# Expert weights with consecutive contraction rows on a partition, and strided stationary tiles to match, in a one-core encoder block

## What is computed

```
def _hier_moe(h, w_rg, b_rg, w_re, b_re, w_gate, w_up, w_down):
    t = h.reshape(b * s, d)                       # 512 tokens x 1024
    g_idx = argmax over 4 groups; top_i = the best 2 of the group's 8 experts
    combine = weight of each token for each of the 32 experts (two are not zero)
    for gi in range(N_EXPERT_GROUPS):
        hg = jnp.einsum('td,edf->tef', t, w_gate[gi])      # 1024 -> 256 per expert
        hu = jnp.einsum('td,edf->tef', t, w_up[gi])
        act = silu(hg) * hu * combine[:, gi, :, None]
        out = out + jnp.einsum('tef,efd->td', act, w_down[gi])   # 256 -> 1024
```

## Time and profile before

| | us |
|---|---|
| median of 3 runs | 947.07 |
| lowest and highest | 946.57, 948.12 |
| span of the profiled execution, first to last instruction | 947.1 |
| PE busy in it | 840.8 |
| expert stage, first fetch to last `down` | 590.5 to 903.0 |

### The profile page before, as it was taken

One profiled execution on the slowest core, in us unless ns is written; L12 is line 12 of the kernel. 1 busy time (PEld: TensorE's weight loads), 2 busy tenths in 40 slices (PEclk: granted clock), 3 DMA queues, 4 the chain that ended last, 5 costly groups with the idle time before them and its releaser, 6 DMA issues.

```text
span 947.1 us, 11294 instructions
## 1 busy us (share of the span) xinstructions
PE 840.8 (89%) x4489; PEld 584.5 (62%) x4489; DVE 426.3 (45%) x780; ACT 176.5 (19%) x331; POOL 151.3 (16%) x74
## 2 busy tenths in 40 slices
PE   0599997799999999999999998999999999999910
PEld 0488787788888885444448887756565556555600
DVE  6999534455688883112365763112111211121128
ACT  4222223453232220000002010111111111111112
POOL 6734741110123111000004000000000000000032
PEclk9999998899999999999999999999999999999965
DMA  9524231111121226230007462359999999999452
GB/s 307 193 90 89 82 97 45 45 45 46 46 78 56 57 78 233 78 126 31 21 0 253 148 206 106 97 201 359 357 357 371 361 360 356 367 363 358 153 183 106
DMA packets 119296, 163.42 MB, mean 173 GB/s; under 512 B 14412, under 2 KB 102614, under 8 KB 118742
## 3 DMA queue, kind: packets, MB, share of 16 engines
q1 hardware_dynamic: 113184, 139.68, 45.1%
q0 software_dynamic: 3072, 12.63, 3.7%
q10 hardware_dynamic: 2998, 10.53, 2.8%
HBM read 148.15 MB, written 14.68 MB: 172 GB/s over the span
## 4 chain that ended last, share of the span: by engine, by line
PE 83%; DVE 8%; DMA 4%; ACT 2%; issue 2%; POOL 0%; ACTq 0%; SPq 0%; DVEq 0%; POOLq 0%
PE psum L732 23%; PE psum L1010 14%; PE psum L1022 12%; PE psum L1037 6%; PE psum L941 6%; PE psum L931 6%; PE psum L980 4%; PE psum L922 3%; DMA ring<-in_w_in_dram 2%; DVE arena L1378 2%; ACT arena L1090 2%; DVE arena L1377 2%; PE psum L871 2%; PE psum L891 1%; PE psum L982 1%
## 5 line engine op out<-in xcount | busy, mean ns | idle before, releaser
L732 PE MATMUL psum<-ring_r 128*128 128x512 f32 (+1 forms) x768 | 213.2, 363 | 2.6 <-DVE arena L1549 1.3
L732 PEld LDWEIGHTS psum<-ring_r 128*128 128x128 f32 x768 | 139.4, 194 | 26.1 <-issue 2.4
L1010 PEld LDWEIGHTS psum<-arena 128*128 128x128 f32 x1088 | 125.5, 194 | 28.4 <-issue 25.1
L1010 PE MATMUL psum<-arena 128*128 128x128 f32 x1088 | 131.6, 280 | 2.9 <-DVE arena L1702 2.9
L667 POOL TENSOR_TENSOR ring_r<-ring,ring_r 128x2048 fp32r<-128x2048 f32 x20 | 93.4, 4670 | 205.3 <-ACT ring_r L1090 205.3
L1090 ACT COPY arena<-psum 128x512 f32<-128x512 f32 (+3 forms) x104 | 58.5, 582 | 351.8 <-PE psum L948 139.8
L1022 PE MATMUL psum<-ring,arena 128*64 128x512 f32 x512 | 113.4, 595 | 7.9 <-ACT arena L1090 7.9
L732 PE MATMUL psum<-arena_r,ring_r 128*128 128x512 f32 x256 | 100.4, 392 | 0.0
L1797 DVE SCALAR_TENSOR_TENSOR arena<-arena,psum 128x256 f32<-128x256 f32 x16 | 6.7, 421 | 186.5 <-ACT arena L1268 186.5
L1022 PEld LDWEIGHTS psum<-ring,arena 128*64 128x64 f32 x512 | 37.1, 137 | 73.9 <-issue 65.5
L695 POOL DMA_INDIRECT ring<-y_rows,rowsU x8 | 8.1, 1017 | 389.4 <-ACT arena L1090 387.2
(11 more groups left out here) (240 smaller groups left out, 875.8 us busy)
## 6 DMA issues: line engine op xcount, KB each, us to landing
ring<-in_w_exp_gate_dram SPq DMA_DIRECT2D x32, 1024.0 KB, 12.1
ring<-in_w_exp_up_dram SPq DMA_DIRECT2D x32, 1024.0 KB, 12.5
ring<-in_w_exp_down_dram SPq DMA_DIRECT2D x32, 1024.0 KB, 9.1
ring<-in_w_in_dram SPq DMA_DIRECT2D x18, 1024.0 KB, 5.3
y_rows<-arena ACTq DMA_DIRECT2D x16, 512.0 KB, 7.6
y_rows<-arena POOLq DMA_DIRECT2D x4, 1024.0 KB, 7.3
ring<-in_w_out_ssd_dram SPq DMA_DIRECT2D x4, 1024.0 KB, 7.4
ring<-in_w_out_dram SPq DMA_DIRECT2D x4, 1024.0 KB, 11.0
```

The lines of the kernel that those rows point to most:

```text
L732: t = mm(o, a, b, start=(first and j == 0), stop=(last and j == 2))
L1010: t = mm(o[:, k, :], h[:, i, c:c + P], onehot[:, buf, i, :], start=(i == 0), stop=(i == NT - 1))
```

## The change

Every contraction tile of the expert weights now holds every eighth row (gate and up) or every second row (down): row `8 p + k` or `2 p + k` lies on partition `p` in tile `k`. The rows of one partition are then consecutive in memory, so it receives one run of 8 KB for each weight. In the same way `fetch` takes as its stationary operand the columns `8 n + k` of `h` (a step of 8 words, 32 bytes, between neighbours) in place of the columns `128 k + n`, and `act_t` the columns `2 n + k` of `eact` (a step of 2 words, 8 bytes). The numbers of instructions, the bytes, the moving operands, the waits and the order stay.

```
--- before.py
+++ after.py
@@ -311,6 +311,8 @@
         xgT = shaped(R_X + 2048, "p (b k t) -> p b k t", b=2, k=KD, t=P)
         eactT = shaped(R_A + 6144, "p (b k t) -> p b k t", b=2, k=2, t=P)
+        h_strided = shaped(R_H, "p (i n k) -> p i k n", i=NT, n=P, k=KD)
+        eact_strided = shaped(R_X + 1024, "p (b n k) -> p b k n", b=2, n=P, k=2)
@@ -563,7 +565,7 @@
-                        src = t[bass.ds(p * 2 + half, 1)].rearrange("a (k p) f -> p (a k) f", p=P)
+                        src = t[bass.ds(p * 2 + half, 1)].rearrange("a (p k) f -> p (a k) f", p=P)
                         slot = expert_slot(u % 2, half, w)
                         sp.dma_start(ring[:, slot], src).then_inc(slot_in[slot], 16)
@@ -572,7 +574,7 @@
-                    src = wd[bass.ds(p * 2 + half, 1)].rearrange("a (k p) n -> p (a k) n", p=P)
+                    src = wd[bass.ds(p * 2 + half, 1)].rearrange("a (p k) n -> p (a k) n", p=P)
                     slot = expert_slot(u % 2, half, 2)
                     sp.dma_start(ringN[:, slot], src).then_inc(slot_in[slot], 16)
...
@@ -1005,9 +1007,9 @@
                 for k in range(4):
-                    c = (4 * part + k) * P
                     for i in range(NT):
-                        t = mm(o[:, k, :], h[:, i, c:c + P], onehot[:, buf, i, :], start=(i == 0), stop=(i == NT - 1))
+                        t = mm(o[:, k, :], h_strided[:, i, 4 * part + k, :], onehot[:, buf, i, :], start=(i == 0),
+                               stop=(i == NT - 1))
@@ -1044,7 +1046,7 @@
                 for k in range(2):
-                    t = tr(o[:, k, :], eact[:, u % 2, k * P:(k + 1) * P], ident)
+                    t = tr(o[:, k, :], eact_strided[:, u % 2, k, :], ident)
```

More of the change, by code:

```diff
@@ L603, in _ @@
                         for w, t in ((0, wg), (1, wu)):
-                            src = t[bass.ds(e, 1)].rearrange("a (k p) f -> p (a k) f", p=P)
+                            src = t[bass.ds(e, 1)].rearrange("a (p k) f -> p (a k) f", p=P)
                             slot = expert_slot(0, half, w)
                             sp.dma_start(ring[:, slot], src).then_inc(slot_in[slot], 16)
-                        src = wd[bass.ds(e, 1)].rearrange("a (k p) n -> p (a k) n", p=P)
+                        src = wd[bass.ds(e, 1)].rearrange("a (p k) n -> p (a k) n", p=P)
                         slot = expert_slot(0, half, 2)
```

## The result

The changed kernel takes 1084.9 us in the median (1082.5 to 1086.3) against 947.6 beside it: 1.144 times the kernel before, 95% interval 1.143 to 1.146. That is 137 us slower. The forecast was 947.1 us, with a rival at 1055 and a range up to 1057; the time lies above all of them.

A forecast was written before the change was run, and what follows sets the result against it. The prediction took PE's chain of work and handover in the expert stage as the bound, loads only keeping up. 947.1 + 0 for loads + 0 for `fetch` and `act_t` = 947.1 us; 8-in-10 range 945 to 1057 us.

The forecast's parts named there:

- a rival at 1055: In `fetch`, a strided load takes two steps per word, 218 ns: 108 us more; chance 0.34 including a milder 1001 us.
- What bounds the kernel: Expert stage: PE's work and one handover set 18.88 us per pair; loads only keep up, and slower `fetch` is paid fully.
- The loads: Expert weights in 8 KB runs: 401 GB/s assumed, 17.0 us of DMA per pair, no gain on the chain.
- The margin at the last load: A pair's last up weight should land some 1.5 to 2.5 us before PE wants it, rather than 0.9.
- rival 4: DMAs are cut into the same pieces as before, time 947.1 us; a small part of the forecast's 0.56.
- rival 2: Expert loads: 8 KB runs move more slowly, at 330 GB/s, and PE waits in `gate_up`: 971 us; chance 0.04.
- The relief of the other engines: Whether lighter DMA traffic by itself helps PE, ACT or DVE: costed at nothing.
- rival 3: ACT's handover shrinks from 0.65 to 0.55 us in all pairs, with fewer instruction waits: 944.6 us; chance 0.06.
- The stationary tiles of `fetch`: 1088 weight loads at a 32-byte step: bounded between nothing and 152 us longer, taken as zero.
- the choice of zero: In `fetch`, a stride halving the read pace gives 0.89 ns per word, a 114 ns load, covered by the matmul's 118.
- The upper bound: In `fetch`, a DVE product's slowdown of 2.36 applied to the load: 258 ns, stage 152 us longer.
- The transposes: In `act_t`, 32 instructions at an 8-byte step: taken as nothing, since two neighbours still lie within 16 bytes.

The follow-up runs named there:

- e1: Changed kernel with contiguous stationary tiles again in `fetch` and the activation transposes, only the weights' 8 KB runs kept: 948.1 us against 948.0 for the kernel before.
- e7: Kernel before with only `fetch`'s stationary operand at a step of 16 words (64 bytes): 1063.3 us.
- e13: Kernel before with only `fetch`'s stationary operand at a step of 32 words (128 bytes): 1062.2 us.
- e5: Kernel before with gate and up weights in 4 KB runs and `fetch`'s stationary operand at a matching step of 4 words: 1078.9 us.
- e2: Kernel before with only `fetch`'s stationary operand at a step of 8 words, weights in the old 1 KB and 4 KB runs: 1084.7 us.
- e4: Kernel before with gate and up weights in 2 KB runs and `fetch`'s stationary operand at a matching step of 2 words: 954.9 us.
- e12: Kernel before with `fetch`'s operands exchanged, the moving `h` taken as two neighbouring words, then a jump by 16: 947.8 us.
- e3: Kernel before with only the activation transposes' stationary operand at a step of 2 words: 948.7 us, ratio 0.9998 to 1.002.
- e6: Kernel before with only `fetch`'s stationary operand at a step of 3 words (12 bytes): 1014.7 us.

## Why the prediction was wrong, point by point

**What bounds the kernel: right.** PE's chain of 18.88 us per pair held, the loads were off it, and no faster load could gain. e1 shows that directly. The remark that whatever slows `fetch` is paid in full is what happened. (The 353 GB/s of its first paragraph is 356 in the earlier trace rows; nothing rests on it.)

**The loads: right in direction, the rate a little low.** 401 GB/s was taken for 8 KB runs. In 5 us of the changed kernel in which long runs and some stores move, the window (last column GB/s) shows 420:

```profile
737.00:742.00 5.00, 4.69 (x22) 1.63 (x24) 0.00 (x0) 0.53 (x2) 0.00 (x0) 1.00 1.01 420
```

The margin at the last load was put at 1.5 to 2.5 us and is 2.9 in e1. The packets fell, so rival 4 is out, and so is rival 2. That landing would come within 10 us of issue was wrong, for the reason told under e1. The relief of the other engines was costed at nothing, and is nothing: rival 3 is out.

**The stationary tiles of `fetch`: here it failed.** The bounds were set at 0 and 152 us, and the truth of 136 lies between them; but the value taken was 0, and the rival's price, 108 us, was too small, so the range ended at 1057. Nothing was left for the stretch from 108 to 152 us, though the working had no argument against it. Two steps are at fault.

The first is the choice of zero. It said that PE reads a moving word every 0.44 ns, and that a stride, if it halved this, would leave a word every 0.89 ns, which is just hidden. The halving had no source, and it is what failed: at a step of 8 words a word came every 244 / 128 = 1.91 ns, not 0.89. In the stream of the earlier trace rows the words are neighbours, four to a line of 16 bytes, so all that it shows of lines is that one comes at least every 227 / 128 = 1.77 ns. Whether lines can come faster than that it doesn't tell, since 227 ns may be the matmul's own pace. If they can't, a load of 128 lines takes 227 ns. So the row that was read as a reason for zero leaves room, as an estimate, for 1088 x (227 - 118) ns, some 119 us. The runs measured 225 (e7, e13), 240 (e5) and 244 ns (e2).

The second is the rival's factor. It doubled the load's 109 ns to 218; the runs show a time that goes by lines and not by a multiple of 109, and 244 is 2.24 times it. The upper bound, 258 ns and 152 us, came closest, but by luck: its factor of 2.36 was that of two DVE products.

The Trainium skill's page "SBUF — State Buffer", Specifications (TRN2), was cited against the change: lines of 16 bytes, and a penalty where every access opens another line. The runs agree with the line length: nearly the full cost at step 4 (240 ns), and with two words on each line almost none (e4 at 124 ns, e12 at 118). It was given the smaller chance because no row showed it.

**The transposes: right in the number, not in the reason.** They cost nothing that can be measured (e3), but the reason given, that two neighbours still lie within 16 bytes, would have left their load as it was, and its row grew by 57 ns. The term is small because there are only 32 of them.

**The chances.** 0.56 was laid on a mechanism for which the only argument was the misread row, against 0.34 for the one that the cited page spoke for.

## What to carry to other kernels

Before an operand of PE is read with a step, count the 16-byte lines that its words touch, and compare lines x 1.9 ns with the time of the matmul that it lies under: here 244 ns disappears under 512 columns (432 ns) and doubles the cost of 128 (118 ns). A layout that gives longer DMA runs is worth that only where a load stands on the chain of waits; full DMA digits beside a full PE don't say so, the releasers and the landing of the last load do. If both are wanted, two neighbouring words per jump keep the read at full pace (shown for a moving operand only), or the stride belongs on an operand whose matmul is long.

## What the runs showed of the hardware

- PE's read of SBUF, stationary or moving, goes by lines of 16 bytes: about 1.9 ns for each line in float32 (stationary, 124 ns for 64, 180 for 96, 240 to 244 for 128; moving, 239 for 128). It is never below the pace of the matmul or load itself (118 and 109 ns for 128 columns; e12's 64 lines under a moving operand stay at 118). At steps of 16 and 32 words it is 1.76 ns (225 ns). The transposes' load, 57 ns more at a step of 2, doesn't fit and stays open.
- The price of 128 lines doesn't change with the granted clock. The stage's first two `fetch` calls come after PE has been idle for 2.87 us, and from 590.5 to 594 us the mean granted clock is 0.67 in the kernel before and 0.58 in the changed one, between its two levels of 1.2 and 2.4 GHz. The next two calls run at 1.00; their chain rows are, before and after the change:

```profile
607.37 7.36 PE psum L1010 x64
613.02 15.45 PE psum L1011 x64
```

  Contiguous, the first two took 9.05 us, 1.69 more; strided, 15.55, 0.10 more. At steps of 2 and 3 words (e4, e6), with fewer lines, they took 9.35 for 7.75 and 12.01 for 11.31, so there the clock still shows.
- Nor does the price differ between 1 KB and 8 KB runs of the loads beside it (7.81 us for a `fetch` in e2, 7.80 in the changed kernel).
- SP is held longer while it issues loads of short runs: 3.3 us at the median for an up weight in 1 KB runs, 0.45 in 8 KB runs (kernel before and changed kernel); for a gate weight 1.23 and 0.33.
